# Eight experts on one core: phases of two jobs taken four up slots, then two down slots

## The chip, the cores and the metric

The kernel runs on one core of a Trainium2 chip. The metric is device time in microseconds (us) of one execution; lower is better. The kernel before took 1402.84 us, the median of three runs (1402.73 to 1404.31).

## The reference

A decoder trunk of two layers over 256 tokens of width 1024, all in float32: an mLSTM layer with a dense SwiGLU, then a sparse-attention layer with a mixture of experts, then a norm. The change touches the mixture of experts only, which takes the second half of the time. What it computes:

```python
D_MODEL, SEQ, N_EXPERTS, TOP_K, FFN_EXPERT = 1024, 256, 8, 2, 3584
logits = t @ w_router
top_v, top_i = lax.top_k(logits, TOP_K)
top_w = jax.nn.softmax(top_v, axis=-1)
gate = jnp.sum(jax.nn.one_hot(top_i, N_EXPERTS, dtype=jnp.float32) * top_w[..., None], axis=1)
gu = jnp.einsum('nd,edf->nef', t, w_gu)
act = jax.nn.silu(gu[..., :FFN_EXPERT]) * gu[..., FFN_EXPERT:] * gate[..., None].astype(t.dtype)
return jnp.einsum('nef,efd->nd', act, w_down)
```

## The kernel before

All weights stream through SBUF in slots of 1 MB (`SLOT`, 128 partitions of 2048 float32). The kernel is written engine by engine, each with its own program, and semaphores alone tie them together. SyncE issues the loads in the order of the slot numbers `n`, each as soon as the buffer that it takes has been used (line 358, `s_used`). There are `RING` = 11 buffers. Slots 0 to 70 belong to the layers before; from `N0` = 71 on the experts follow.

An expert is a *job* of 28 up slots (`w_gu`) and 14 down slots (`w_down`). Jobs come in two kinds. An **A job** has room for 128 tokens. Its float32 products are made of three matmuls in the float32r format (`mm3`, lines 1539 to 1541): high by high, high weights by low part and low by high. So its weights must be *split*: ScalarE copies the slot into one of `SPLIT` = 4 buffers `w_hi` (line 839), and VectorE subtracts that from the slot in place, which gives `w_lo` (line 1438). A slot is 12 matmuls of 512 columns, for up (`gu`, kind 0) and for down (`down_part`, kind 0). A **B job** has room for 64 tokens (`CAP_B`). It takes the loaded slot as it is, in float32, and runs two 64-column halves of the array side by side: 16 matmuls of 256 columns for an up slot (line 2039), 8 of 512 for a down slot (line 2060), as the trace counts them (it has two records for each matmul of the code).

The jobs overlap in *phases*. The first is the up part of an A job alone (below and in the prediction "phase 0"). Then rounds of two phases follow: one with `up` = 1, the up part of a B job beside the down part of the A job before, and one with `up` = 0, the up part of the next A job beside the down part of the B job. There are three rounds with these inputs. A last phase up 1 and the 14 down slots of the last B job end it. A phase with two jobs takes two up slots, then one down slot, 14 times (`m` in the loops, `c, h = divmod(m, 2)`). `h` = 0 fills bank 0 with the gate half of chunk `c`, `h` = 1 bank 1 with the up half. ScalarE makes the silu of bank 0 (`sg`, line 871; `sgb` of B), VectorE the product (`av`, line 1451; `avb`), TensorE transposes the product (`turned`, line 2087; `turned_b`, line 2098) one chunk later, and ScalarE and VectorE copy it out as `at_hi` and `at_lo`, the stationary operand of the down part.

Each engine's program has the same loop over `m`. On ScalarE and VectorE the loop's step begins with `split(last + AHEAD)`: it splits all slots of A up to three beyond the last slot of this step, then does the step's silu or product. A split of slot `n` on ScalarE waits for its landing and for the use of the slot that had the same `w_hi` buffer, the fourth slot of A before it (`hi_free`):

```python
if is_split(n):
    act.wait_ge(landed[buffer(n)], landing(i, n))
    act.wait_ge(s_used, hi_freed(i, n))
    a(w_hi[:, hi_order(n) % SPLIT, :], slot_raw(n), ACT.Copy).then_inc(s_hi, 1)
```

Between the steps stand the pieces for the jobs to come: `places` (one-hot and gates turned), `gather`, `gather_b` and `gather_t`, `gather_bt` (the tokens of the next job into its rows, and turned). At the end of a phase TensorE first takes two up slots of the next phase, then scatters the finished job's rows back to the tokens with four one-hot products into the banks `scatter_banks`, and VectorE adds each bank to `xs` (line 1504). The next phase waits for the third of these adds ahead of its step `m` = 1 (bank 1), and for the fourth ahead of `m` = 2. After a phase up 1, VectorE makes `y_lo` (line 1496), then the splits up to four slots into the next phase, then the adds.

## Time and profile before

| | |
|---|---|
| median of three runs | 1402.84 us |
| the profiled execution | 1403.82 us |
| its span | 1402.1 us |
| TensorE busy, matmuls | 1359.9 us (97%) |
| VectorE, ScalarE busy | 797.9 us (57%), 677.3 us (48%) |
| loads of expert slots | 247 + 89, 1 MB each |

The span is the time from the first to the last record of the core. A busy share is a mean over stages with different limits, and matmuls are pipelined, so their busy time overlaps: the spacing of their starts tells more than the length of one. The granted clock is 1.0 or 0.5 of 2.4 GHz. The chain of work that ended last, followed backwards, says which engine or load was waited for; the timelines say when each instruction started and, in brackets, how long its engine had been idle and who ended that.

### The profile page before, as it was taken

Reading aid. Unit: us, or ns where it says so; the run is one execution under the profiler, and the core shown is the slowest. Engines: PE = TensorE matmul, PEld = TensorE weight load, DVE = VectorE, ACT = ScalarE, POOL = GpSimd, SP = SyncE. Lnnn points to the kernel's source line nnn. Section 1 sums busy time; section 2 is a strip of 40 time slices with the busy share of each in tenths; the row PEclk is TensorE's granted clock in tenths of the full one; section 3 lists DMA queues with packets and bytes.
Section 4 is the critical chain, followed back from the end, with each engine's and each line's share of the span. In section 5 each row is a group of like instructions: output and inputs, shape, how many; then the busy total and the mean of one; then the engine's idle time right before and its main releaser. Section 6 shows DMA issues by size and latency. Waiting matters only on the chain.

```text
span 1402.1 us, 19231 instructions
## 1 busy us (share of the span) xinstructions
PE 1359.9 (97%) x7452; PEld 983.1 (70%) x7452; DVE 797.9 (57%) x880; ACT 677.3 (48%) x834; POOL 40.8 (3%) x96
## 2 busy tenths in 40 slices
PE   7999999998999989999999999999999999999987
PEld 7987888887985467776666666666666666666652
DVE  6946655546858858862475653366643357654332
ACT  6546544435657846743354633355543345533221
POOL 7000000001000000000000000000000000000000
PEclk9999999999999999999999999999999999999999
DMA  8443555454632046999999979999999999989996
GB/s 356 170 156 144 181 181 188 173 202 152 219 148 90 1 165 236 337 372 422 420 421 421 398 299 421 421 421 420 420 360 422 421 420 421 422 355 418 421 421 277
DMA packets 59993, 431.69 MB, mean 308 GB/s; under 512 B 6656, under 2 KB 6656, under 8 KB 7808
## 3 DMA queue, kind: packets, MB, share of 16 engines
q1 hardware_dynamic: 59760, 429.95, 77.0%
q8 instruction: 60, 0.98, 0.3%
q10 hardware_dynamic: 144, 0.52, 0.1%
q14 instruction: 29, 0.24, 0.0%
HBM read 429.40 MB, written 1.05 MB: 307 GB/s over the span
## 4 chain that ended last, share of the span: by engine, by line
PE 86%; DMA 9%; DVE 2%; ACT 2%; issue 0%; POOL 0%; SPq 0%; POOLq 0%; DVEq 0%; ACTq 0%
PE bank L1539 20%; PE bank L1541 19%; PE bank L1540 19%; PE bank L2039 10%; DMA raw<-in_moe 8%; PE bank L2060 6%; PE bank L1887 2%; PE bank L1913 2%; PE bank L1986 1%; PE bank L1897 1%; PE bank L2087 1%; DVE w_lo L1438 1%; ACT w_hi L839 1%; PE bank L1915 1%; PE bank L1994 1%; DVE ht_lo L979 0%
## 5 line engine op out<-in xcount | busy, mean ns | idle before, releaser
L1438 DVE TENSOR_TENSOR w_lo<-raw,w_hi 128x2048 fp32r<-128x2048 f32 x117 | 266.5, 2290 | 178.7 <-ACT w_hi L839 178.4
L1539 PE MATMUL bank<-w_hi,ht_hi 128*128 128x512 f32 (+1 forms) x768 | 303.0, 395 | 0.9 <-DVE ht_lo L979 0.9
L1541 PE MATMUL bank<-w_hi,ht_lo 128*128 128x512 f32 (+1 forms) x768 | 296.5, 386 | 0.0
L839 ACT ACTIVATE w_hi<-raw 128x2048 fp32r<-128x2048 f32 x117 | 222.6, 1917 | 129.7 <-DMA raw<-in_moe 99.9
L1540 PE MATMUL bank<-w_lo,ht_hi 128*128 128x512 f32 (+1 forms) x628 | 241.5, 385 | 0.0
L947 DVE TENSOR_TENSOR w_lo<-raw,w_hi 128x2048 fp32r<-128x2048 f32 x73 | 166.7, 2290 | 109.7 <-ACT w_hi L515 109.5
L515 ACT ACTIVATE w_hi<-raw 128x2048 fp32r<-128x2048 f32 x74 | 141.5, 1919 | 94.6 <-PE bank L1541 92.8
L1539 PEld LDWEIGHTS bank<-w_hi,ht_hi 128*128 128x128 f32 x768 | 144.3, 188 | 56.6 <-issue 26.6
L1541 PEld LDWEIGHTS bank<-w_hi,ht_lo 128*128 128x128 f32 x768 | 144.3, 188 | 29.9
L2039 PE MATMUL bank<-raw,xb 128*64 128x256 f32 x1344 | 156.0, 382 | 0.0
L1539 PE MATMUL bank<-w_hi,at_hi 128*128 128x512 f32 x312 | 128.1, 411 | 9.7 <-DVE w_lo L1438 8.5
L2039 PEld LDWEIGHTS bank<-raw,xb 128*64 128x64 f32 x1344 | 92.9, 137 | 58.5 <-issue 16.3
L1540 PEld LDWEIGHTS bank<-w_lo,ht_hi 128*128 128x128 f32 x628 | 118.1, 188 | 21.8
L1438 DVE TENSOR_TENSOR more_lo<-more,w_hi 128x2048 fp32r<-128x2048 f32 x47 | 107.3, 2289 | 44.8 <-ACT w_hi L839 44.6
L839 ACT ACTIVATE w_hi<-more 128x2048 fp32r<-128x2048 f32 x47 | 89.9, 1914 | 74.3 <-DMA more<-in_moe 61.8
L1541 PE MATMUL bank<-w_hi,at_lo 128*128 128x512 f32 x312 | 122.6, 393 | 0.0
L1540 PE MATMUL bank<-w_lo,at_hi 128*128 128x512 f32 x264 | 103.7, 393 | 0.0
L1539 PEld LDWEIGHTS bank<-w_hi,at_hi 128*128 128x128 f32 x312 | 58.8, 188 | 33.2 <-DVE w_lo L1438 13.4
L2060 PE MATMUL bank<-raw,at_b 128*64 128x512 f32 x336 | 80.0, 603 | 0.5 <-DMA raw<-in_moe 0.5
L1541 PEld LDWEIGHTS bank<-w_hi,at_lo 128*128 128x128 f32 x312 | 58.9, 189 | 13.0
L852 ACT ACTIVATE sgb<-bank 128x256 f32<-128x256 f32 x28 | 10.7, 383 | 108.3 <-PE bank L2039 108.3
L871 ACT ACTIVATE sg<-bank 128x512 f32<-128x512 f32 x28 | 16.7, 596 | 91.0 <-PE bank L1541 91.0
(336 smaller groups left out, 1664.6 us busy)
## 6 DMA issues: line engine op xcount, KB each, us to landing
raw<-in_moe SPq DMA_DIRECT2D x247, 1024.0 KB, 14.1
more<-in_moe SPq DMA_DIRECT2D x89, 1024.0 KB, 15.7
raw<-in_wts SPq DMA_DIRECT2D x71, 1024.0 KB, 4.9
xs<-in_x SPq DMA_DIRECT2D x2, 512.0 KB, 4.1
out<-xn SPq DMA_DIRECT2D x4, 256.0 KB, 2.0
pk<-in_packed SPq DMA_DIRECT2D x1, 517.0 KB, 7.6
g1b<-in_norm_ffn ACTq DMA_DIRECT2D x1, 512.0 KB, 3.5
gfb<-in_norm_final SPq DMA_DIRECT2D x1, 512.0 KB, 18.8
```

The source lines that it names most:

```text
L515: a(w_hi[:, n % SPLIT, :], slot_raw(n), ACT.Copy).then_inc(s_hi, 1)
L839: a(w_hi[:, hi_order(n) % SPLIT, :], slot_raw(n), ACT.Copy).then_inc(s_hi, 1)
L871: a(sg[:, 0, :], B[0][:, :], ACT.Silu).then_inc(s_silu, 1)
L947: v.tensor_tensor(slot_lo(n), slot_raw(n), w_hi[:, n % SPLIT, :].bitcast(F32), ALU.subtract).then_inc(s_lo, 1)
L1438: v.tensor_tensor(slot_lo(n), slot_raw(n), w_hi[:, hi_order(n) % SPLIT, :].bitcast(F32), ALU.subtract).then_inc(s_lo, 1)
L1539: mm(out_, sh, mh, start=first, stop=False)
L1540: mm(out_, sh, ml, start=False, stop=False)
L1541: return mm(out_, sl, mh, start=False, stop=last)
L1887: mm(B[n % 3][:, 0:2 * lk], qt[lo:lo + 64, h // 2, t * P:(t + 1) * P], kt[lo:lo + 64, :, h // R, 0:lk], start=True, stop=True).then_inc(s_ ...
L1913: mm(bank[0:64, :], vv[:, k, b, g * DB:(g + 1) * DB], ptg[grp % 2][:, j, :, :] .rearrange("p r q -> p (r q)"), start=j == 0, stop=False)
L2039: ins = mm(bank[64 * side:64 * side + 64, 0:256], xb[:, kk, :], weights(raw, n, 512)[:, k, 256 * side:256 * side + 256], start=kk == 0, st ...
L2060: ins = mm(B[to][64 * side:64 * side + 64, :], at_b[:, 2 * d + k, :], weights(raw, n, 1024)[:, k, 512 * side:512 * side + 512], start=d == ...
```

## The change

Two job phases take four up slots, then two down slots, seven times, in place of two and one fourteen times. The number of matmuls, splits and loads stays, their order changes on every engine and in the order of the loads. The transposes, places and gathers move so that each stands beside 128-column work where there is some. The first phase (up part alone) keeps its order on TensorE; there and elsewhere the split runs up to `MOE_AHEAD` = 5 slots beyond the step's last slot, and no further than slot `length + 1`, instead of `AHEAD` = 3.

```diff
--- before.py
+++ after.py
@@ -41,6 +41,7 @@
 XW = 2 * 16 * G * NC_ + 12
 XM = G * NC_ + 12
 AHEAD = 3
+MOE_AHEAD = 5
 SC = 4
 TURN = 4
 
@@ -241,8 +242,8 @@
         r, m = divmod(n - N0 - UP_SLOTS, 2 * JOB_SLOTS)
         if r < 0:
             return n
-        d = max(m - JOB_SLOTS, 0)
-        return N0 + UP_SLOTS + r * JOB_SLOTS + min(m, JOB_SLOTS) // 3 + 2 * (d // 3) + d % 3
+        b, d = min(m, JOB_SLOTS), max(m - JOB_SLOTS, 0)
+        return N0 + UP_SLOTS + r * JOB_SLOTS + 2 * (b // 6) + max(b % 6 - 4, 0) + 4 * (d // 6) + min(d % 6, 4)
 
     def is_split(n):
         return splits_before(n + 1) > splits_before(n)
@@ -334,13 +335,13 @@
 
     def up_slot(c, h, u, paired):
 
-        return (3 if paired else 2) * (2 * c + h) + u
+        return (6 if paired else 4) * c + 2 * h + u
 
     def column(job):
         return slice(job, job + 1) if isinstance(job, int) else bass.ds(job, 1)
 
     def down_slot(d, paired):
-        return 3 * d + 2 if paired else d
+        return 6 * (d // 2) + 4 + d % 2 if paired else d
 
     def scatter_banks(late):
 
@@ -371,13 +372,14 @@
         def phase_loads(i, first, up, down):
 
             n = first
-            for d in range(DOWN_SLOTS):
+            for c in range(DOWN_SLOTS // 2):
                 if up is not None:
-                    for u in range(2):
-                        load(n, job_slot(bass.ds(up, 1), 2 * d + u), i)
+                    for u in range(4):
+                        load(n, job_slot(bass.ds(up, 1), 4 * c + u), i)
                         n += 1
-                load(n, job_slot(bass.ds(down, 1), UP_SLOTS + d), i)
-                n += 1
+                for d in (2 * c, 2 * c + 1):
+                    load(n, job_slot(bass.ds(down, 1), UP_SLOTS + d), i)
+                    n += 1
 
         def expert(col):
             return sp.value_load(tab[0:1, column(col)], min_val=0, max_val=NE - 1)
@@ -864,27 +866,23 @@
                         turned_b(6)
                     continue
                 last = up_slot(c, h, 1, paired)
+                split(min(last + MOE_AHEAD, length + 1))
                 if up == 0 and h == 0:
-                    split(last + AHEAD)
                     used(last)
                     act.wait_ge(s_mul, (i + up_plus) * 7 + (12 + c))
                     a(sg[:, 0, :], B[0][:, :], ACT.Silu).then_inc(s_silu, 1)
                     if c:
                         high_a(c - 1, up_plus)
                 elif up == 0:
-                    split(last + AHEAD)
                     if c == 0 and down == 1:
                         turned_b(6)
                 elif h == 0:
-                    split(last + AHEAD)
-                    if c == 0:
-                        high_a(6, 0)
                     used(last)
                     silu_b(c)
-                    if c:
-                        turned_b(c - 1)
+                elif c:
+                    turned_b(c - 1)
                 else:
-                    split(last + AHEAD)
+                    high_a(6, 0)
                 if m == 3 and down is not None:
                     places_copied(i * 2 + (down + 1), up)
                 if gather is not None:
@@ -892,12 +890,10 @@
                         rows_b_copied(B[7], i + up_plus)
                     if up == 0 and m == gather + 5:
                         gathered_b(B[7], i + up_plus)
-                    if up == 1 and m in (gather + 3, gather + 4):
-                        gathered_rows(m - gather - 3, B[7], i + 1)
-                    if up == 1 and m in (gather + 5, gather + 7):
-                        gathered_high((m - gather - 5) // 2, B[7], i + 1)
-            if up is not None:
-                split(length - 1 + AHEAD)
+                    if up == 1 and m in (gather + 3, gather + 5):
+                        gathered_rows((m - gather - 3) // 2, B[7], i + 1)
+                    if up == 1 and m in (gather + 7, gather + 9):
+                        gathered_high((m - gather - 7) // 2, B[7], i + 1)
             if down is not None:
                 act.wait_ge(s_gc, i * 2 + (down + 1))
                 if down == 0:
@@ -1462,19 +1458,15 @@
                 if up is None:
                     continue
                 last = up_slot(c, h, 1, paired)
+                split(min(last + MOE_AHEAD, length + 1))
                 if up == 0 and h == 0:
-                    split(last + AHEAD)
                     if c:
                         low_a(c - 1, up_plus)
                 elif up == 0:
-                    split(last + AHEAD)
                     product_a(c)
-                elif h == 0:
-                    split(last + AHEAD)
+                elif h == 1:
                     if c == 0:
                         low_a(6, 0)
-                else:
-                    split(last + AHEAD)
                     product_b(c)
                 if down is None and m < 3:
                     job_tables(6 + 2 * m)
@@ -1484,10 +1476,8 @@
                         if down is not None:
                             dve.wait_ge(s_gs, i * 2 + (down + 2))
                         one_hot(column(gather_job), P if up else CAP_B)
-                    if m in (gather + 5, gather + 7) and up == 1:
-                        gathered_low((m - gather - 5) // 2, B[7], i + 1)
-            if up is not None:
-                split(length - 1 + AHEAD)
+                    if m in (gather + 7, gather + 9) and up == 1:
+                        gathered_low((m - gather - 7) // 2, B[7], i + 1)
             if down is not None:
                 if down == 0:
                     dve.wait_ge(s_gc, i * 2 + 1)
@@ -2098,48 +2088,55 @@
                     ins = nc.tensor.transpose(B[4 + c % 2][:, b * P:(b + 1) * P], avb[:, c % 2, b * P:(b + 1) * P], ident[:])
                 ins.then_inc(s_bt, 1)
 
-            for m in range(DOWN_SLOTS):
-                c, h = divmod(m, 2)
-                if up is not None:
-                    if m == 1 and down is not None:
+            for c in range(DOWN_SLOTS // 2):
+                if up is None:
+                    if c == 0:
+                        turned_b(6)
+                    else:
+                        for d in (2 * c, 2 * c + 1):
+                            down_part(i, first + d, d, 1, 0)
+                    continue
+                for h in range(2):
+                    if c == 0 and h == 1 and down is not None:
                         pe.wait_ge(s_xu, i * 8 + (4 * down + 11))
-                    if m == 2 and down is not None:
+                    if c == 1 and h == 0 and down is not None:
                         pe.wait_ge(s_xu, i * 8 + (4 * down + 12))
                     if c and up == 0:
                         pe.wait_ge(s_mul if h else s_silu, (i + up_plus) * 7 + (12 + c))
                     elif c:
                         pe.wait_ge(s_bact if h else s_bsilu, i * 7 + c)
-                    for u in range(2):
-                        if m:
-                            gu(i, first + up_slot(c, h, u, paired), 2 * m + u, B[h], up)
-                    if h == 0 and c and up == 0:
+                    if c or h:
+                        for u in range(2):
+                            gu(i, first + up_slot(c, h, u, paired), 2 * h + u, B[h], up)
+                    if c and h == 0 and up == 0:
                         turned(c - 1, up_plus)
-                    if m == 0 and up == 1:
+                    if c == 0 and h == 0 and up == 1:
                         turned(6, 0)
-                    if h == 0 and c and up == 1:
-                        turned_b(c - 1)
-                if m == 0 and down == 1:
+                    if c == 1 and h == 0 and up == 0 and paired:
+                        places(i * 2 + (down + 1))
+                if up == 0 and c == 0 and paired:
                     turned_b(6)
-                if up is None and m >= 2:
-                    down_part(i, first + down_slot(m, paired), m, down, 0)
-                elif paired:
-                    down_part(i, first + down_slot(m, paired), m, down)
-                if m == 2 and paired:
+                if up == 0 and gather_at is not None and c == 3:
+                    gather_bt(B[7], i + up_plus)
+                if up == 1 and c:
+                    turned_b(c - 1)
+                if up == 1 and c == 1:
                     places(i * 2 + (down + 1))
+                if paired:
+                    for d in (2 * c, 2 * c + 1):
+                        down_part(i, first + down_slot(d, paired), d, down)
                 if gather_at is not None:
-                    if up == 0 and m == gather_at + 2:
+                    if up == 0 and c == 2:
                         gather_b(B[7], gather_job)
-                    if up == 0 and m == gather_at + 4:
-                        gather_bt(B[7], i + up_plus)
-                    if up == 1 and m == gather_at + 2:
+                    if up == 1 and c == 2:
                         gather(0, B[7], gather_job)
-                    if up == 1 and m == gather_at + 3:
+                    if up == 1 and c == 3:
                         pe.wait_ge(s_gr, i * 2 + 3)
                         gather(1, B[7], gather_job)
-                    if up == 1 and m == gather_at + 4:
+                    if up == 1 and c == 4:
                         pe.wait_ge(s_gr, i * 2 + 4)
                         gather_t(0, B[7], i + 1)
-                    if up == 1 and m == gather_at + 6:
+                    if up == 1 and c == 5:
                         pe.wait_ge(s_gal, i * 2 + 3)
                         gather_t(1, B[7], i + 1)
             if following == "last":
```

## Rows read from the trace of the kernel before

**Rows 1.** The page, its part 4: shares of the chain by engine.

```profile
PE 86%; DMA 9%; DVE 2%; ACT 2%; issue 0%; POOL 0%; SPq 0%; POOLq 0%; DVEq 0%; ACTq 0%
```

**Rows 2.** The chain in order of time: start, us, engine, target, line.

```profile
1118.76 19.40 DMA raw<-in_moe
...
1140.20 2.30 DVE w_lo L1438
...
1371.26 17.90 DMA raw<-in_moe
```

**Rows 3.** Busy time by stretch: PE, PEld, DVE, ACT, POOL, PEclk, DMA share, GB/s.

```profile
800.00:820.00 20.00, 20.00 (x92) 13.13 (x90) 11.06 (x8) 9.61 (x8) 0.00 (x0) 1.00 0.56 210
1020.00:1040.00 20.00, 20.00 (x89) 13.87 (x88) 10.28 (x6) 8.69 (x7) 0.00 (x0) 1.00 0.84 333
```

**Rows 4.** Timeline of TensorE, up 0 and last phase: start, us, engine, line, operation.

```profile
804.84 0.50 PE L1539 MATMUL bank<-w_hi,ht_hi 128*128 128x512 f32 x1
...
810.61 1.94 PE L2060 MATMUL bank<-raw,at_b 128*64 128x512 f32 x8
812.48 0.50 PE L1539 MATMUL bank<-w_hi,ht_hi 128*128 128x512 f32 x1
...
1376.06 1.89 PE L2060 MATMUL bank<-more,at_b 128*64 128x512 f32 x8
1377.78 6.61 PE L2060 MATMUL bank<-raw,at_b 128*64 128x512 f32 x30
```

**Rows 5.** Timeline of TensorE, phase 0: transposes of two chunks, first matmul between.

```profile
599.17 0.60 PE L2087 MATMUL bank<-ident,av 128*128 128x128 f32 x4
599.53 0.48 PE L1539 MATMUL bank<-w_hi,ht_hi 128*128 128x512 f32 x1
...
610.52 0.60 PE L2087 MATMUL bank<-ident,av 128*128 128x128 f32 x4
```

**Rows 6.** Timeline of TensorE, phase up 1: B, B, A, then B again.

```profile
836.70 1.95 PE L2039 MATMUL bank<-raw,xb 128*64 128x256 f32 x16
838.47 1.90 PE L2039 MATMUL bank<-more,xb 128*64 128x256 f32 x16
840.30 0.50 PE L1539 MATMUL bank<-w_hi,at_hi 128*128 128x512 f32 x1
...
843.24 1.08 PE L2039 MATMUL bank<-raw,xb 128*64 128x256 f32 x8
```

**Rows 7.** Timeline of ScalarE, phase 0: table load, a split, silu and `at_hi`.

```profile
539.46 1.28 ACT L871 ACT_TABLE_LOAD   x1
...
596.70 1.92 ACT L839 ACTIVATE w_hi<-raw 128x2048 fp32r<-128x2048 f32 x1 [0.80 <-PE bank L1541]
599.37 0.60 ACT L871 ACTIVATE sg<-bank 128x512 f32<-128x512 f32 x1 [0.75 <-PE bank L1541]
599.87 0.59 ACT L847 ACTIVATE at_hi<-bank 128x512 fp32r<-128x512 f32 x1
```

**Rows 8.** Timeline of VectorE, phase 0: split, product, splits.

```profile
593.62 2.29 DVE L1438 TENSOR_TENSOR w_lo<-raw,w_hi 128x2048 fp32r<-128x2048 f32 x1
595.82 0.68 DVE L1451 TENSOR_TENSOR av<-sg,bank 128x512 f32<-128x512 f32 x1
596.41 4.53 DVE L1438 TENSOR_TENSOR w_lo<-raw,w_hi 128x2048 fp32r<-128x2048 f32 x2
```

**Rows 9.** Timelines of VectorE and TensorE at the border from up 1 to up 0.

```profile
1147.73 1.41 DVE L1496 SCALAR_TENSOR_TENSOR y_lo<-bank,gcol,y_hi 128x512 fp32r<-128x512 f32 x2
...
1152.37 2.47 DVE L1504 TENSOR_TENSOR xs<-xs,bank 128x512 f32<-128x512 f32 x4
...
1152.80 0.38 PE L2098 MATMUL bank<-ident,avb 128*128 128x128 f32 x2
```

**Rows 10.** Busy time by stretch, ahead of the first expert job (columns as before).

```profile
520.00:525.00 5.00, 1.88 (x16) 1.28 (x13) 3.70 (x17) 2.27 (x5) 0.40 (x1) 0.88 0.88 370
525.00:530.00 5.00, 3.57 (x7) 1.89 (x7) 4.39 (x29) 2.19 (x2) 0.00 (x0) 0.50 0.00 0
```

## Prediction

> **What bounds the kernel now.** Read the page's share line of the chain that ended last first: TensorE carries 86% of it, DMA 9% [rows 1]. Then the chain in order of time: it leaves TensorE for a load at 1118.76 and 1371.26 us, and at 1140.20 it comes back through the VectorE split of that weight slot [rows 2]. So both take turns. The table by stretches shows where: TensorE is busy for all 20 us of 800 to 820 and of 1020 to 1040, and the DMA share falls there to 0.56 and 0.84 [rows 3]. These are the ends of phases of kind up 0 (A up, B down), where the ring of buffers is full and loads wait for TensorE. From such an end to the last stretch of the next up 1 phase (B up, A down) the DMA engines set the pace; then a phase of kind up 0 is TensorE's again. The last load sets the end.
>
> Four stretches of TensorE are thus on the path: from the first expert job (534 us) through its own phase (up 0 alone, called phase 0 here), a phase up 1 and a phase up 0, all without a wait for data; and later the two further phases of kind up 0. What TensorE saves or loses there moves the end one for one. What it saves in the other phases of kind up 1 is lost to the wait for the load.
>
> **Fewer changes of form (saves).** A phase with two jobs alternates between 128-column and 64-column weights 14 times now and 7 times after. Phase up 0: from 804.84 to 812.48 stand two A slots and one B slot, 7.64 us [rows 4]. Twelve A matmuls without a change take (610.52 - 599.53)/4 = 2.75 us, less 0.02 for the first after transposes, so 2.73 [rows 5]. A B down slot in a run of its own kind takes 1377.78 - 1376.06 = 1.72 us [rows 4]. The pair of changes costs 7.64 - 2 x 2.73 - 1.72 = 0.46 us. The nearest lower bound is B's own excess, (812.48 - 810.61) - 1.72 = 0.15 us [rows 4]. Part of the excess is a slower pace inside the A slots, so I take 0.40: 7 x 0.40 = 2.8 us a phase (1.1 to 3.2). Phase up 1: two B slots take 3.60 us from 836.70, the second 0.06 longer than the first, and the A slot behind them 843.24 - 840.30 = 2.94 us against 2.73 [rows 6]. A pair costs 0.06 + 0.21 = 0.27 us, 7 x 0.27 = 1.9 us. The Trainium skill, "TensorEngine Tiling (Array Packing)", Key Properties, says that changing the tiling mode drains the engine; rows 6 agree that it costs something, and show how little.
>
> The transposes, places and gathers are the same instructions at new places; each already stood at a border between runs or inside a 128-column run, so I cost the move at nothing (0.1 us each way a phase).
>
> **The split runs further ahead (costs).** This is the edit that decides. ScalarE and VectorE work strictly in the order of their program. AHEAD = 3 becomes MOE_AHEAD = 5, and the split still stands in front of the silu (ScalarE) and of the product (VectorE). `w_hi` has four buffers: slot n can be split only when slot n - 4 of A has been used. In phases with two jobs, A's slot 6c+8 takes the buffer of 6c+2, used long before. But phase 0 has A's slots alone, four for each chunk c. There, at (c, h = 1), VectorE must now split slot 4c+8 before the product of chunk c, and ScalarE's half of that split waits until TensorE has used slot 4c+4, which belongs to the next chunk. TensorE wants the product right after slot 4c+5, for `turned(c)`. Count from the start of slot 4c+4:
> - it is used at 2.72; ScalarE starts about 0.3 later and takes 1.92 (now, too, the split at 596.70 starts upon a release by TensorE, with 0.80 us of idle time before it, one slot of 2.72 us ahead of the transposes at 599.17: 0.25 behind the end of the slot before [rows 5, 7]);
> - VectorE takes 2.20 for its half (593.62 to 595.82) and 0.60 to the end of the product (595.82 to 596.41) [rows 8]; a release to TensorE costs some 0.1. Sum 7.85 us.
> - TensorE is ready at 2 x 2.72 = 5.44. It idles 2.4 us. Now there is no such gap in front of 599.17 or 610.52 [rows 5].
>
> The silu moves too: it now waits for the split of 4c+6, that is for slot 4c+2. Counted from the start of slot 4c+2, 2.72 + 0.3 + 1.92, 0.50 for the silu itself (599.37 to 599.87 [rows 7]) and 0.1 for the release give 5.54 us, where slot 4c+4 would start at 5.44: another 0.1 to 0.3 us. Chunks 1 to 4 pay some 2.6 us each, 10.4 us. Chunk 0 pays more, since ScalarE's load of the silu table, 1.28 us [rows 7], comes behind the wait: 2.6 + 1.3 = 3.9 us. Chunk 5 pays only the silu's 0.2, since slot 28 is B's and isn't split. **Phase 0 loses 10.4 + 3.9 + 0.2 = 14.5 us** (12 to 17: 4 x 2.2 + 3.2 at the low end, where a release is quicker; 4 x 3.1 + 4.6 at the high end, where waits of a gather are added). Nothing covers it: TensorE is the path here, and the loads of this stretch wait for TensorE too. Queued behind the waiting split on ScalarE are the silu, `at_hi`, `rows_b`; on VectorE the product and `at_lo`.
>
> **The border from up 1 to up 0 (costs).** Slots of bank 1 wait for the third of VectorE's four adds that empty the scatter banks. Now one B slot stands in front of that wait and covers it. After the change slots (0, h = 1) follow the scatter at once. Besides, the next phase begins A A A A, so both slots 2 and 3 are split between `y_lo` and the adds, where now it is one. In the row: `y_lo` ends at 1149.1, one split (2.2 [rows 8]), then four adds from 1152.37 at 0.62 each; the scatter ends at 1152.80 [rows 9]. With two splits behind `y_lo` (1149.6 after the extra work in front) the adds start at 1154.1 and the third ends at 1156.0, where TensorE is ready at 1153.05: 2.95 us idle. Where the phase before wasn't held by loads (the first of the three borders) the splits are earlier and it is 1.6 us. Behind a DMA-held phase the last A slots and the gathered low half cost 0.25 us more.
>
> **The sum on the path.** Phase 0: +14.5. First phase up 1: -1.9. First phase up 0: -2.8 + 1.65. The two later phases up 0: each -2.8 + 2.95 + 0.25 = +0.4. Total 14.5 - 1.9 - 1.15 + 0.8 = **+12.3 us** (rounded up from 12.25). The number and bytes of loads don't change, and the order of loads follows the use; the last phase (14 B down slots) is held by loads until the end and keeps its tail: cost nothing, and the cover is thin: a delay of TensorE by more than a microsecond there would be late next.
>
> The profiled run took 1403.82 us with a span of 1402.1; the median of the three runs is 1402.84, 1.0 lower. I put the sum on the median: 1402.84 + 12.3 = 1415.1 us.
>
> **Rivals.**
> - *The waits of phase 0 don't bite* (the split finds its buffer in time, so the silu and product come as now). For it: ScalarE has idle time between its splits [rows 7]. Against: that idle time is no room, as a release by TensorE ends it; the split further ahead asks for a later release. Then the sum is -1.9 - 1.15 + 0.8 = -2.2 us: 1400.6. This is the case on the faster side, and it decides from the point at which the product is ready 5.44 us after slot 4c+4's start. Chance 0.10, about evenly faster and the same (a saving of 2.2 lies just within 0.2%; with 0.46 a pair and a shorter border wait it is 4 us).
> - *The changes of form weren't what the excess is*: with two A slots and four B slots in a row the pace stays, and nothing is saved. Then 14.5 + 1.65 + 2 x 3.2 = 22.6 us: 1425. Against: the same instruction is quicker in a run of its kind [rows 4, 6]. Chance 0.05.
> - *The clock falls.* In front of the first expert job TensorE was busy for 1.88 us of 5 us, and in the next 5 us the granted clock was 0.50, the 1.2 GHz level [rows 10]. The new waits repeat five times in phase 0 and thrice at borders, each behind dense work. A fall as long as that row's 5 us costs 2.5 us of matmul time; three of them 7.5 us: 1422.6. It decides from the first wait in phase 0 after which 1.2 GHz is granted. Chance 0.10. The Trainium skill, "TensorE: Matmul & The Clock Gate", The HAM clock gate, says the same of cause: the throttled state is the default and activity lifts it; whether gaps of 2.5 us inside dense work suffice, no row here shows.
>
> **How the numbers follow.** Forecast 0.75, its own range 1410 to 1420. Range of 8 in 10: from 1408 (the waits half as long: 14.5 becomes 7.3) to 1422 (three clock drops, or half of the saving missing). Left out: the first rival and part of the others. A measurement of this kernel can tell about 0.2%, 2.8 us, from no change. Faster 0.05, same 0.05, slower 0.90.
>
> **What would show it.** In the trace of after: in phase 0, idle TensorE of about 2.5 us ahead of the transposes of `av`, ended by the product on VectorE, five times, with a distance of 13.5 to 14 us (more where a gather stands between) between transposes where now it is 11.35; silu starts behind two splits, not one; up 0 slots 2 and 3 preceded by 1.5 to 3 us idle, ended by `xs`; A slot pairs of 2.94 + 2.73 us in phases up 1; the span of a phase up 0 shorter by 2 to 3 us apart from that border. Wrong if the distance in phase 0 stays near 11.4 us, if the clock column shows 0.5 in it, or if a phase up 0 gets slower by other waits, such as the product behind the split of slot 6c+8.

## The result and the profile after

The kernel after took 1428.42 us (median of four runs, 1421.17 to 1429.3), beside 1402.78 us before (four runs, 1402.3 to 1404.31). The ratio is 1.0169, 95% interval 1.0135 to 1.0204: it is slower by some 25 us (25.6 by the medians, 24 by the ratio), twice the 12.3 that were forecast. The profiled execution took 1429.3 us with a span of 1427.5, so the difference between the two spans is 25.4 us.

The page of after, its shares of the chain by engine (part 4):

```profile
PE 78%; DMA 11%; DVE 5%; ACT 3%; issue 2%; POOL 0%; DVEq 0%; SPq 0%; POOLq 0%; ACTq 0%
```

Against [rows 1] TensorE gave up eight points of the chain, to VectorE, ScalarE, the loads and to "issue". In order of time (start, us, engine, target, line) the chain shows what has come in between. Cuts from it: the transposes of the second and of the third product of phase 0 with what stands ahead of the third, and one row of the last border:

```profile
572.15 0.68 PE bank L2077 x4
...
586.85 2.15 issue
589.00 0.69 DVE av L1447
589.73 1.11 PE bank L2077 x4
1176.85 1.90 DVE xs L1494 x3
```

Two consumers of VectorE's results now hold TensorE up that did not before: the transposes in phase 0 wait for the product `av`, and the third A slot after a border waits for the adds to `xs`. The waits of TensorE over the experts of after (530 to 1430 us), grouped: engine, target and line, who was waited for, us in total, times, the longest:

```profile
PE bank L2077 <- DVE av L1447: 12.1, 5, 3.1
PE bank L1529 <- DVE w_lo L1434: 10.6, 10, 1.8
PE bank L1529 <- DVE xs L1494: 6.2, 3, 2.4
...
PE bank L1529 <- ACT sg L873: 1.3, 1, 1.3
...
PE bank L2004 <- ACT rows_b L809: 0.7, 1, 0.7
```

The five waits for `av`, the one for the silu (`sg`) and the one for `rows_b` all lie in phase 0. What made a product late is in the timelines of ScalarE, VectorE and TensorE around 587 us (start, us, engine, line, operation, and in brackets the idle time before and who ended it):

```profile
584.84 1.92 ACT L841 ACTIVATE w_hi<-more 128x2048 fp32r<-128x2048 f32 x1 [2.90 <-PE bank L1531]
...
586.79 2.29 DVE L1434 TENSOR_TENSOR more_lo<-more,w_hi 128x2048 fp32r<-128x2048 f32 x1 [2.49 <-ACT w_hi L841]
589.00 0.68 DVE L1447 TENSOR_TENSOR av<-sg,bank 128x512 f32<-128x512 f32 x1
...
587.07 0.39 PE L1531 MATMUL bank<-w_hi,ht_lo 128*128 128x512 f32 x1
589.73 1.11 PE L2077 MATMUL bank<-ident,av 128*128 128x128 f32 x4 [2.27 <-DVE av L1447]
590.50 0.78 PE L1529 MATMUL bank<-w_hi,ht_hi 128*128 128x512 f32 x1
591.07 0.63 PE L1530 MATMUL bank<-w_lo,ht_hi 128*128 128x512 f32 x1
591.50 0.63 PE L1531 MATMUL bank<-w_hi,ht_lo 128*128 128x512 f32 x1
...
606.70 1.07 PE L2077 MATMUL bank<-ident,av 128*128 128x128 f32 x4 [2.25 <-DVE av L1447]
```

ScalarE is idle for 2.90 us until a matmul of the next chunk releases `w_hi`, splits for 1.92 us, VectorE is idle until then, splits its half for 2.2 us and only then makes the product. TensorE has been without work since 587.46. That is the chain of the forecast. What its sum did not have is in the rows from 591.07 on: behind the wait matmuls that were 0.39 us long and 0.23 apart at 587 take 0.63 us and start 0.43 apart. The table by stretches of after (PE, PEld, DVE, ACT, POOL, granted clock, DMA share, GB/s) names the reason:

```profile
586.00:589.70 3.70, 1.46 (x7) 0.88 (x5) 2.91 (x3) 2.67 (x2) 0.00 (x0) 1.00 0.84 325
589.70:593.10 3.40, 3.37 (x10) 2.88 (x11) 2.18 (x1) 0.00 (x0) 0.00 (x0) 0.50 0.59 243
593.10:600.00 6.90, 6.17 (x29) 4.74 (x29) 2.89 (x2) 5.18 (x5) 0.00 (x0) 1.00 0.57 203
606.80:610.20 3.40, 3.40 (x11) 2.82 (x12) 2.04 (x1) 0.00 (x0) 0.00 (x0) 0.50 0.56 236
```

For 3.4 us after the wait the granted clock is 0.50, the 1.2 GHz level. In this execution it falls behind four of the five waits for `av` (at 556, 573, 590 and 607 us; not behind the fifth, which ends at 622.27), twice at borders (962 and 1180 us), and twice in the last phase up 1 (1337 and 1368 us), behind waits for `w_lo` of 1.78 and 1.83 us.

So the difference can be told by phases. The table has the time from the first matmul of a phase to the first of the next in the profiled executions, from the timelines of TensorE; look3 is the experiment below that has the change without its phase 0. The last two rows part at the last matmul of an A job and end with the last down matmul of B.

| phase | before | after | look3 |
|---|---|---|---|
| phase 0 (up part alone) | 82.19 | 104.57 | 82.09 |
| first up 1 | 98.13 | 95.83 | 95.81 |
| first up 0 | 113.13 | 112.44 | 112.42 |
| up 1 | 102.14 | 103.18 | 102.64 |
| up 0 | 113.13 | 114.97, clock fell | 113.42 |
| up 1 | 102.25 | 102.57 | 103.56 |
| up 0 | 113.13 | 114.93, clock fell | 114.91, clock fell |
| last up 1 | 104.01, clock fell | 103.28, clock fell twice | 103.27, clock fell |
| last 14 down slots | 28.0 | 28.9 | 28.9 |

The differences of after, by row: +22.4, -2.3, -0.7, +1.0, +1.8, +0.3, +1.8, -0.7, +0.9; with the start of the first expert matmul 0.9 us later (535.3 instead of 534.4) the sum is 25.4, the difference of the spans. The falls in the last phase up 1 leave no mark in it: it waits for loads, and is 0.7 us shorter with two falls than before with one.

### The profile page after: what moved, and what is told of

It is laid out like the page before. It is cut to its first block, busy times and chain, and to the rows that moved or that the text cites. A ratio compares the mean times of both kernels' runs of the same rounds, so it can differ in the third digit from the quotient of the medians.

```text
span 1427.5 us, 19226 instructions
## 1 busy us (share of the span) xinstructions
PE 1360.2 (95%) x7452; PEld 996.7 (70%) x7452; DVE 795.1 (56%) x880; ACT 674.8 (47%) x834; POOL 40.5 (3%) x96
## 4 chain that ended last, share of the span: by engine, by line
PE 78%; DMA 11%; DVE 5%; ACT 3%; issue 2%; POOL 0%; DVEq 0%; SPq 0%; POOLq 0%; ACTq 0%
PE bank L1529 19%; PE bank L1531 18%; PE bank L1530 18%; DMA raw<-in_moe 9%; PE bank L2029 7%; PE bank L2050 6%; PE bank L1877 2%; PE bank L1903 2%; ACT w_hi L841 2%; DVE w_lo L1434 1%; DMA more<-in_moe 1%; PE bank L1887 1%; PE bank L1976 1%; PE bank L2077 1%; DVE xs L1494 1%
## 5 line engine op out<-in xcount | busy, mean ns | idle before, releaser
L1434 DVE TENSOR_TENSOR w_lo<-raw,w_hi 128x2048 fp32r<-128x2048 f32 x130 | 296.7, 2291 | 260.7 <-ACT w_hi L841 260.0
L841 ACT ACTIVATE w_hi<-raw 128x2048 fp32r<-128x2048 f32 x130 | 248.0, 1916 | 272.6 <-DMA raw<-in_moe 171.7
L1530 PE MATMUL bank<-w_lo,ht_hi 128*128 128x512 f32 (+1 forms) x664 | 258.2, 389 | 0.0
L943 DVE TENSOR_TENSOR w_lo<-raw,w_hi 128x2048 fp32r<-128x2048 f32 x73 | 166.6, 2290 | 109.7 <-ACT w_hi L517 109.5
L517 ACT ACTIVATE w_hi<-raw 128x2048 fp32r<-128x2048 f32 x74 | 141.4, 1918 | 95.5 <-PE bank L1531 92.8
L2029 PE MATMUL bank<-raw,xb 128*64 128x256 f32 x1280 | 147.1, 381 | 1.8 <-DVE xs L1494 1.8
L1530 PEld LDWEIGHTS bank<-w_lo,ht_hi 128*128 128x128 f32 x664 | 126.6, 191 | 23.7
L841 ACT ACTIVATE w_hi<-more 128x2048 fp32r<-128x2048 f32 x34 | 65.1, 1915 | 85.1 <-DMA more<-in_moe 59.3
L1434 DVE TENSOR_TENSOR more_lo<-more,w_hi 128x2048 fp32r<-128x2048 f32 x34 | 77.8, 2289 | 48.7 <-ACT w_hi L841 48.4
L2050 PE MATMUL bank<-raw,at_b 128*64 128x512 f32 x264 | 61.1, 598 | 0.6 <-DMA raw<-in_moe 0.5
L1530 PEld LDWEIGHTS bank<-w_lo,at_hi 128*128 128x128 f32 x280 | 53.3, 191 | 10.6
L2029 PE MATMUL bank<-more,xb 128*64 128x256 f32 x512 | 59.3, 379 | 0.0
```

What stands on the lines that cost most here:

```text
L517: a(w_hi[:, n % SPLIT, :], slot_raw(n), ACT.Copy).then_inc(s_hi, 1)
L943: v.tensor_tensor(slot_lo(n), slot_raw(n), w_hi[:, n % SPLIT, :].bitcast(F32), ALU.subtract).then_inc(s_lo, 1)
L1434: v.tensor_tensor(slot_lo(n), slot_raw(n), w_hi[:, hi_order(n) % SPLIT, :].bitcast(F32), ALU.subtract).then_inc(s_lo, 1)
L1530: mm(out_, sh, ml, start=False, stop=False)
L2029: ins = mm(bank[64 * side:64 * side + 64, 0:256], xb[:, kk, :], weights(raw, n, 512)[:, k, 256 * side:256 * side + 256], start=kk == 0, st ...
L2050: ins = mm(B[to][64 * side:64 * side + 64, :], at_b[:, 2 * d + k, :], weights(raw, n, 1024)[:, k, 512 * side:512 * side + 512], start=d == ...
```

## The experiments

### look3 and only5: is it phase 0, and is it the look-ahead?

**look3** keeps everything of the change, but the first phase splits three slots ahead as before. **only5** is the kernel before, and its first phase alone splits five ahead.

```diff
 # look3, from after, on ScalarE and on VectorE
-                split(min(last + MOE_AHEAD, length + 1))
+                split(min(last + (MOE_AHEAD if paired else AHEAD), length + 1))
 # only5, from before, each split of a step on ScalarE and VectorE
-                    split(last + AHEAD)
+                    split(last + (AHEAD if paired else 5))
```

> The changed kernel with the split's look-ahead of 3 slots instead of 5 in the phase that has no down part; everything else stays. Theory 1 (look-ahead in front of silu and product makes TensorE wait, and the waits lower the clock): the five waits ahead of the transposes of av and the four stretches at the 1.2 GHz level in that phase go, some 22 us, leaving the saved changes of form against the border waits: 1402.8 - 5.4 (first two job phases) + 2.4 + 2 x 2 = 1404, range 1401 to 1408. Theory 2 (the order of four and two itself costs, through bursts in which the buffers come free): it stays above 1420.

> The kernel before with one part of the change alone: look-ahead of 5 slots instead of 3 in the phase without a down part. Theory 1: that phase gets 22 us longer with four falls of the clock, 1425; 15 us without the falls, 1418. Theory 2: within 3 us of 1402.8.

look3 took 1405.92 us (ten runs, 1403.61 to 1408.49), 1.0013 of before (0.9998 to 1.0029). only5 took 1422.01 us (four runs, 1418.12 to 1425.12), 1.0123 of before (1.0097 to 1.0149). The kernel before beside them took 1403.39 us. Their first phases in the tables by stretches, first look3's, then only5's:

```profile
534.40:616.50 82.10, 82.10 (x374) 66.17 (x374) 69.91 (x60) 58.57 (x44) 0.00 (x0) 1.00 0.88 338
```

```profile
534.00:638.50 104.50, 90.31 (x375) 70.28 (x374) 72.60 (x61) 56.49 (x44) 0.00 (x0) 0.93 0.70 266
```

In look3 TensorE is busy without a gap at full clock, as before. In only5 the phase takes 104.5 us at a mean clock of 0.93, and the waits of TensorE in it (530 to 650 us) are those of after:

```profile
PE bank L2087 <- DVE av L1451: 12.2, 5, 3.2
PE bank L1539 <- ACT sg L871: 1.3, 1, 1.3
PE bank L2014 <- ACT rows_b L807: 0.7, 1, 0.7
```

One constant in one phase gives 22.3 us there with the old order of slots, and taking it away from the change gives 22.5 back. The reordering itself, with all phases of two jobs in it, costs 1.8 to 2.5 us, and its interval (0.3 us less to 4.1 us more than before) includes no cost at all. The expectation of look3 held; only5 came out 3 us under the value of the theory with falls of the clock in it, and 4 above the one with waits alone; its profiled execution (1424.21 us) has four falls in phase 0, as after has. The four runs lie at both values, and their mean granted clock goes with them: 1418.12 and 1419.81 us at 0.992 and 0.993, 1424.21 and 1425.12 at 0.989 and 0.988. So, by their mean clock, the median stands between runs with more falls and runs with fewer. And of the 22.3 us of phase 0 the span shows 20.3 (1422.4 against 1402.1): the last phase up 1 and the last down slots, where TensorE waits for loads, are together 1.4 us shorter than before.

### fill0: what the clock's share of phase 0 is

The waits and the falls behind them come together, so they are parted by keeping TensorE at work in the wait. In front of each wait for a product in phase 0 stand nine matmuls more, of 0.23 us each, into a bank that nobody reads (the output doesn't depend on them).

```diff
 # in turned(c), from after
+                if down is None and c < 5:
+                    for _ in range(9):
+                        mm(B[3][:, :], ht_hi[:, 0, 0:P], ..., start=True, stop=True)
                 pe.wait_ge(s_mul, (i + plus) * 7 + (12 + c + 1))
```

> The changed kernel with nine matmuls of 512 columns more in each of five chunks of the phase without a down part, put where TensorE waits for the product; their result goes to a bank that isn't used there, so the output is unchanged. They take 9 x 0.23 = 2.1 us, no longer than the wait of 2.2 to 3.1. Theory 1 with the clock as part of it: waits for the product end at the same distance from the split as before, but no stretch at 1.2 GHz in that phase, so 4 x 1.7 = 6.8 us less than the changed kernel, about 1421.5. Rival (the falls lie in the shadow of the waits and cost nothing by themselves, or they come from elsewhere): 1428, unchanged, or the falls stay.

It took 1420.94 us (five runs, 1420.14 to 1427.88), 1.0122 of before (1.0105 to 1.0139): with 45 matmuls *more* it is 7.5 us quicker than after. Timeline of TensorE of fill0 at the fourth product, then its table over the phase:

```profile
604.59 2.20 PE L2073 MATMUL bank<-ht_hi 128*128 128x512 f32 x9
607.00 0.66 PE L2080 MATMUL bank<-ident,av 128*128 128x128 f32 x4 [0.21 <-DVE av L1447]
607.41 0.47 PE L1529 MATMUL bank<-w_hi,ht_hi 128*128 128x512 f32 x1
607.72 0.39 PE L1530 MATMUL bank<-w_lo,ht_hi 128*128 128x512 f32 x1
...
540.30:638.70 98.40, 94.50 (x420) 73.85 (x419) 70.51 (x60) 58.34 (x45) 0.00 (x0) 1.00 0.75 282
```

TensorE still gets its transposes only when the product is there, but the matmuls behind them run at 0.39 us and the clock is 1.00 throughout. The phase takes 98.34 us instead of 104.57: four falls cost 6.2 us, 1.56 each. (The profiled execution of fill0 is its slowest, 1427.88 us: its first expert matmul starts at 540.33, 5.9 us later than before, ahead of anything that was changed. Of the others none is over 1422.07.) What is left above 82.19 are the waits, 16.15 us. So in the profiled executions phase 0's 22.4 us are 16.2 of waits and 6.2 of clock.

### prod1st_b and look4: the place and the length of the look-ahead

If the cause is that a split stands in front of the product for which it has no need, then the product moved ahead of the last two splits must be cured of it with the look-ahead left at five. look4 has look3's edit with 4 in place of `AHEAD`.

```diff
 # prod1st_b, from after, VectorE only
+                if down is None and h == 1:
+                    split(last + AHEAD)
+                    product_a(c)
                 split(min(last + MOE_AHEAD, length + 1))
 ...
-                    product_a(c)
+                    if down is not None:
+                        product_a(c)
 # look4, from look3, on ScalarE and on VectorE
-                split(min(last + (MOE_AHEAD if paired else AHEAD), length + 1))
+                split(min(last + (MOE_AHEAD if paired else 4), length + 1))
```

> The changed kernel with VectorE's product moved ahead of the two last splits of its step, in the phase without a down part only; the look-ahead stays 5 and ScalarE's program stays. Theory 1: the waits for the product go (12 us) and the clock stays up (6.8), the silu still comes 0.2 to 1.3 us late per chunk, and w_lo of the slots behind comes in time: 1409, range 1406 to 1413. Rival (the look-ahead itself, not its place, costs): above 1420.

> As look3, but with a look-ahead of 4 slots in the phase without a down part. The count of the prediction gives the product 5.1 us after the start of the chunk's last up slot's successor, and TensorE asks for it after 5.44: no waits, same as look3 within 1.5 us. Rival (each slot further ahead costs its share, so half of the loss of 5 against 3): 8 to 10 us above look3.

prod1st_b took 1409.15 us (seven runs, 1404.91 to 1410.13), 1.0041 of before (1.0027 to 1.0056). Phase 0 takes 85.08 us, and the waits of TensorE in it (530 to 650 us) have no line for `av` left. The two longest:

```profile
PE bank L1533 <- ACT sg L873: 1.3, 1, 1.3
PE bank L2008 <- ACT rows_b L809: 0.7, 1, 0.7
```

The place of the product on VectorE, ahead of two splits instead of behind them, takes away 19.5 of the 22.4 us, and no fall of the clock is left in the phase. The rest is ScalarE's, whose silu and `rows_b` still stand behind the longer look-ahead.

look4 took 1407.93 us (ten runs, 1406.28 to 1409.97), 1.0037 (1.0026 to 1.0049), its phase 0 83.76 us. TensorE waits for one product in it, 1.2 us, that of the second chunk, where VectorE has 1.4 us of small table work in front of the splits (557.91 to 559.34). That phase is 1.7 us longer than look3's 82.09, and the medians are 2.0 apart, a little over the 1.5 within which it was expected to be the same; its profile also has a fall at both later borders, where look3's has one. So four ahead costs one wait in the whole phase and five costs one in each of the first five chunks: by the count in the prediction the step is where the split in front of a product first asks for the buffer of a slot that belongs to the *next* chunk.

### fillb: the clock at the borders

fill0's edit at another place: from look3, nine such matmuls in front of the wait at each border from up 1 to up 0.

```diff
 # from look3, in the loop of TensorE
+                    if c == 0 and h == 1 and down == 1 and up == 0:
+                        for _ in range(9):
+                            mm(B[3][:, :], at_hi[:, 0:P], at_hi[:, 0:4 * P], start=True, stop=True)
                     if c == 0 and h == 1 and down is not None:
                         pe.wait_ge(s_xu, i * 8 + (4 * down + 11))
```

> As look3, with nine matmuls of 512 columns more (2.05 us, into a bank that isn't used there) in front of TensorE's wait for the adds at each of the three borders from up 1 to up 0. Theory 1 with the clock: the wait itself ends where it did, no stretch at 1.2 GHz falls there, and each phase up 0 behind a load-held phase takes 113.4 us, as that of look3 without a fall, not 114.9: 1.5 to 3 us less than look3. Rival (the fall at a border comes from the gaps in the phase up 1 before it, not from this wait): the falls stay, the phases stay at 114.9.

It took 1404.22 us (ten runs, 1402.08 to 1407.92), 0.9999 of before (0.9987 to 1.0012). The clock falls at no border, and the two later phases up 0 take 113.4 and 113.3 us where look3 has 113.42 (no fall) and 114.91 (a fall). In after itself the clock fell at both. Its last border, first VectorE, then TensorE, then the table by stretches:

```profile
1171.13 1.41 DVE L1486 SCALAR_TENSOR_TENSOR y_lo<-bank,gcol,y_hi 128x512 fp32r<-128x512 f32 x2
1172.44 4.49 DVE L1434 TENSOR_TENSOR w_lo<-raw,w_hi 128x2048 fp32r<-128x2048 f32 x2
1176.85 2.48 DVE L1494 TENSOR_TENSOR xs<-xs,bank 128x512 f32<-128x512 f32 x4
...
1176.20 0.40 PE L2175 MATMUL bank<-y_lo,selt 128*128 128x512 f32 x1
1178.86 0.49 PE L1529 MATMUL bank<-w_hi,ht_hi 128*128 128x512 f32 x1 [2.26 <-DVE xs L1494]
...
1180.43 0.63 PE L1529 MATMUL bank<-w_hi,ht_hi 128*128 128x512 f32 x1
...
1175.00:1180.00 5.00, 2.74 (x12) 1.91 (x12) 4.33 (x5) 1.27 (x1) 0.00 (x0) 1.00 1.02 424
1180.00:1185.00 5.00, 5.00 (x17) 3.93 (x16) 4.19 (x2) 4.32 (x4) 0.00 (x0) 0.66 1.01 421
```

Two splits (4.49 us) stand between `y_lo` and the adds, TensorE idles 2.26 us behind its last scatter product at 1176.20, starts at 1178.86, and at 1180.4 the clock is down. The extra matmuls fill the wait; the wait's own time they leave. That they buy the 1.5 us of a fall is not shown here: prod1st_b has the same waits without them (2.36 and 2.30 us), no fall either, and phases up 0 of 113.37 and 113.28 us. What both show is the length of such a phase without a fall. In the profiles of after, look3, look4, fill0 and prod1st_b the clock fell behind seven of ten such waits, so that none fell in fillb's two can be chance. Nor do the intervals part fillb (0.9987 to 1.0012) from look3 (0.9998 to 1.0029). In phase 0 the same remedy stands on firmer ground: eight falls behind ten unfilled waits in after and only5, none behind the five of fill0.

### bank1 and both1: the wait at the border taken away

bank1, from look3, scatters into bank 1 first, so that the slots that need bank 1 wait for the first of the four adds and not for the third. both1, from bank1, also leaves only one split ahead of the adds and puts the second behind the first add.

```diff
 # bank1, from look3
-        return (6, 7, 5, 2) if late else (6, 7, 1, 5)
+        return (6, 7, 5, 2) if late else (1, 6, 7, 5)
 ...
-                        pe.wait_ge(s_xu, i * 8 + (4 * down + 11))
+                        pe.wait_ge(s_xu, i * 8 + (4 * down + 9))
 # both1, from bank1, VectorE
-                    split(length - 1 + TURN)
+                    split(length - 1 + AHEAD)
 ...
-                        split(length - 1 + min(AHEAD + n, TURN))
+                        split(length - 1 + TURN)
```

> As look3, but the scatter fills bank 1 first, and TensorE's wait ahead of the next phase's third and fourth up slots is for the first of the adds instead of the third. Theory 1 (the border wait is the two splits of VectorE that stand in front of the adds): the wait behind a phase up 1 falls by two adds, 1.25 us, from 2.3 to 1.0, at three borders, and the waits of 0.7 at the other borders go: 3 to 4 us less than look3, 1402; with a fall of the clock less 4 to 6. Rival (the border wait is covered, the end is set by loads): same as look3.

> As bank1, and VectorE makes only one of the two splits ahead of the adds, the other behind the first add. Theory 1: no wait at the borders at all, no fall of the clock there, and what is left is the saving of the changes of form: 7 x (0.33 + 0.44 + 0.37 + 0.36) = 10.5 us below the kernel before less about 0.5 for the later last A slots: 1393, range 1390 to 1397. Rival (the saving of form is given back to the loads): 1400 or more.

bank1 took 1399.58 us (ten runs, 1397.52 to 1402.87), 0.9971 of before (0.9958 to 0.9984); both1 1396.7 us (five runs, 1394.82 to 1397.16), 0.9952 (0.9934 to 0.9969). TensorE's waits for the adds over the experts (530 to 1400 us), first look3's, then bank1's; both1 has no such line:

```profile
PE bank L1529 <- DVE xs L1494: 6.2, 3, 2.4
```

```profile
PE bank L1529 <- DVE xs L1494: 2.6, 3, 1.2
```

The last border of both1, VectorE, then TensorE:

```profile
1142.70 2.28 DVE L1434 TENSOR_TENSOR w_lo<-raw,w_hi 128x2048 fp32r<-128x2048 f32 x1
1145.58 0.69 DVE L1494 TENSOR_TENSOR xs<-xs,bank 128x512 f32<-128x512 f32 x1 [0.59 <-PE bank L2175]
1146.18 2.28 DVE L1434 TENSOR_TENSOR w_lo<-raw,w_hi 128x2048 fp32r<-128x2048 f32 x1
1148.38 1.88 DVE L1494 TENSOR_TENSOR xs<-xs,bank 128x512 f32<-128x512 f32 x3
...
1146.43 0.39 PE L2175 MATMUL bank<-y_lo,selt 128*128 128x512 f32 x1
1146.66 0.39 PE L1529 MATMUL bank<-w_hi,ht_hi 128*128 128x512 f32 x1
```

The A slot follows the scatter without a gap. The three phases up 0 take 112.42, 113.42, 114.91 us in look3, 111.22, 112.17, 112.08 in bank1 and 110.60, 110.69, 110.70 in both1. From look3 to bank1 that is 5.3 us, of which 1.5 are the fall of the clock that doesn't come any more, and from bank1 to both1 another 3.5. By the phases bank1's expectation held, in its branch with a fall less (4 to 6 us); by the medians it is 6.3 us less than look3, a little more. TensorE's three waits of some 0.6 us for the adds at the borders to phases up 1 are gone in bank1 too, but those phases wait for loads and did not get shorter (103.0 us on the mean in bank1, 103.2 in look3). both1's median lies 3 to 4 us above the value named, inside its range; its profiled execution (1394.82 us) was the quickest of the five, and the phases held by loads stay as long as they were (103.0 us on the mean, 102.8 before).

both1 is **a version that beats both kernels**: in full it is the change with four edits (look-ahead of three in the first phase, bank 1 scattered first, the wait for it on the first add, one split moved behind that add). Measured a second time:

> The same kernel as both1, for a closer interval against the kernel before: 1395 to 1397, 0.4 to 0.6% below. If its gain was that of one chip and one hour only, within 0.2% of the kernel before.

It took 1396.99 us (nine runs, 1395.3 to 1402.78) beside 1403.5 of before, 0.9961 (0.9945 to 0.9977): 5.5 to 6.7 us or 0.4 to 0.5% quicker than before (by the two ratios), and 31 us quicker than after.

## Why the prediction was wrong

The direction and the chain of waits were right; the clock behind them, and so the size, was not: 1415.1 us, with a range to 1422, against 1428.42.

**The step that failed is the rival "the clock falls".** It was given a chance of 0.10 and left out of the sum, because no row showed a fall behind a wait in the middle of dense work; [rows 10] had one ahead of the first expert only. But the trace of before has such a fall. In the last phase up 1, TensorE's timeline, then the table by stretches:

```profile
1358.78 0.50 PE L1539 MATMUL bank<-w_hi,at_hi 128*128 128x512 f32 x1 [2.32 <-DVE w_lo L1438]
...
1360.00:1363.50 3.50, 3.50 (x10) 2.22 (x11) 0.75 (x1) 0.98 (x2) 0.00 (x0) 0.52 1.02 424
```

A wait of 2.32 us, as long as those that the forecast counted on, and from 1360.1 us on the clock is down. TensorE waits for loads in this phase, so what the fall cost there is not shown. In the profiled execution of after the clock fell six times on the path: four times in phase 0 at 1.56 us, twice at borders at 1.5, together 9.2 us (the rival had three falls of 2.5 us, 7.5 in all). The forecast had eight waits of 1.6 to 3 us behind dense work in it, so whether the clock reacts was the largest open term, and it could only cost. The sum and the clock together would have given 1415.1 + 9.2 = 1424.3, still 4 us low. By the spans, of the 13.2 us that the sum (12.25) lacks to 25.4, 9.2 are the clock, 1.7 the waits of phase 0, 1.8 the later start and the longer tail (0.9 each), 0.6 the phases held by loads; the other rows differ by 0.1 together. The high end of 1422 held the falls alone, without the upper ends of the waits.

**The waits in phase 0: right chain, 14.5 us forecast, 16.2 measured** (fill0's 98.34 - 82.19), inside the step's own range of 12 to 17. Four of the waits for `av` are 2.21 to 2.28 us, forecast 2.4 (its terms add up to 7.84 us, not 7.85). Chunk 0's table load of the silu came as a wait of 1.3 us, as forecast, and `rows_b` as 0.7 us, which was named as queued behind the split but priced only in the high end. The second wait for `av` is 3.12 us, 0.8 more: VectorE has 1.4 us of small table work of the first chunks (565.56 to 567.01) in front of the splits there, which the step did not count. The idle times come to 14.1 us in all. The other 2 us: set beside look3 matmul by matmul, the starts of fill0 slip by 15.2 us at these seven waits, some 0.16 us more at each than the idle time in brackets in after, which is counted from the end of a matmul that overlaps the next one's start (0.39 us long, 0.23 apart). The rest, 1.0 us, are steps of 0.11 us and less, most of them right behind the waits. The silu's 0.2 us for each later chunk do not show as waits of their own. The distance between two transposes was forecast as 13.5 to 14 us, more with a gather: it is 589.73 - 572.15 = 17.6 us with eight matmuls of a gather (1.9 us) in it, and 606.70 - 589.73 = 17.0 with others, since each holds a fall and a wait. The clock column of 0.5 in phase 0, named as what would make the prediction wrong, is what did.

**Fewer changes of form: right in size.** The first phase up 1 saved 2.3 us (forecast 1.9), 0.33 for a pair of changes instead of 0.27. Phase up 0: both1's is free of border waits, 110.6 against 113.13 is 2.5 us, 0.36 a pair; forecast 2.8 at 0.40. The rival that nothing is saved falls. The move of the transposes, places and gathers, priced at nothing, is in both numbers; no run parts it from the forms. In the timeline of TensorE of after, four B slots in a row of a phase up 1, and two B slots of a phase up 0, read:

```profile
666.95 5.40 PE L2029 MATMUL bank<-raw,xb 128*64 128x256 f32 x48
672.18 1.90 PE L2029 MATMUL bank<-more,xb 128*64 128x256 f32 x16
674.01 0.44 PE L2088 MATMUL bank<-ident,avb 128*128 128x128 f32 x2
...
799.12 3.65 PE L2050 MATMUL bank<-more,at_b 128*64 128x512 f32 x16
802.71 0.50 PE L1529 MATMUL bank<-w_hi,ht_hi 128*128 128x512 f32 x1
```

Four B slots take 674.01 - 666.95 = 7.06 us, 1.77 each, against 1.83 for the second of a pair and 1.77 for the first in [rows 6]. Two down slots of B take 3.59 us, 1.80 each, where one alone took 1.87 [rows 4].

**The border: near for the wait, short by the clock.** Forecast was 1.65 us for the first and 2.95 + 0.25 for each of the others, set against the saving of 2.8. In after TensorE is idle for 1.5, 2.4 and 2.3 us there; with a saving of 2.5, what the borders cost comes to 1.8, 2.8 and 2.8 us. No run shows the 0.25 by itself. The first phase up 0 came out 0.7 us shorter (2.5 saved, 1.8 lost). A later phase without a fall came out 0.3 us longer than before (look3's 113.42 against 113.13), forecast 0.4; one with a fall 1.8 longer.

**The phases held by loads:** the sum has nothing for them (its 0.25 for the last A slots stands in the later phases up 0); here +1.0 and +0.3, and the last one -0.7. In nine profiles with the new order the three later phases up 1 take 103.1 us on the mean, in the two with the old (before and only5) 102.35. With single values from 101.49 to 104.01 in those two alone that is a hint of 0.75 us a phase, whose cause stays open. The 0.9 us at the start and the 0.9 at the end are not the new order's: look3, which has it, starts at 534.4 as before does, and only5, which has the old one, has a tail of 29.1 us too.

**The rival on the faster side** (waits don't bite, 1400.6) is the sum without phase 0. look3 is that kernel, and took 1405.92. By its profile (span 1402.9 against 1402.1) phase 0, the first up 1 and the three up 0 give -1.0 us, with one border's fall of the clock in them (-2.5 without), where the sum had -2.2; the phases held by loads, the start and the tail make up the rest. So even this rival would have been no gain that can be measured: the border gives back what the forms save.

## What to carry to other kernels

A split, a prefetch or any producer that is to run further ahead on an in-order engine must not stand in front of a result that its consumer needs before it releases the buffer. Count which slot's use it waits for: if that use lies behind the result still to be made, a longer look-ahead is a stall in every round. Price a new wait on TensorE in dense work with the loss of clock behind it, here two thirds again of a 2.3 us wait (1.56 us), and look for falls in the whole trace of before, not only on its path. When work is regrouped, look at what stood as cover for the waits at the borders: the forms saved 2.3 + 3 x 2.5 = 9.8 us on the path here, and it took the order in which four banks are scattered and added (from look3 to both1 9.2 us) to keep it.

## What the hardware showed that was not expected

- A wait of 2.25 us in the middle of a stretch in which TensorE was busy throughout can bring the granted clock to 0.50 for 3.4 us, at a cost of 1.5 to 1.6 us. The Trainium skill, "TensorE: Matmul & The Clock Gate", The HAM clock gate, has the throttled state as the default that activity lifts; the trace agrees, and puts waits as short as this among those that count. In the phases held by loads waits of 1.65 to 1.83 us did it too (both1 at 1318 us, look3 at 1343, after at 1337 and 1368).
- Not each such wait does it. In phase 0 of after and of only5 the clock fell behind four of five waits, not behind the last (2.28 us in after, where 2.21 and 2.25 brought one); in look3 behind a border wait of 2.29 us, not behind the one of 2.38 in the border before, and in prod1st_b behind neither; a wait of 1.5 us at the first border never did in any profile. What decides between equal waits is open.
- Idle TensorE time filled with nine matmuls of 0.23 us, whose result nobody reads, kept the clock at 1.00 in phase 0: 98.34 us instead of 104.57. At the borders the same filling (113.4 us instead of 114.91 for a phase) can't be told from chance.
- The same kernel does not fall equally often in each run. The run of after that took 1421.17 us had a mean granted clock of 0.990, the three of 1427.74 to 1429.3 us one of 0.984 or 0.985; only5 shows the same. In which phase the falls were missing is not shown, as the profile is of one execution of each kernel.
